# A mixer's score stage in another order: one cin chunk between the heads' and the sample's scores, exponentials before the v path on ScalarE

## The reference

```
ua, va, q, k, v, cin, gb, gc, gates = project(rmsnorm(x), w_in)
vn = rmsnorm(gelu(va), g_v)                     # the "v path" of branch A
A  = gelu(ua) * (W_s . vn + b_s)                # spatial mixing within 128 rows
B  = softmax(q k^T / 8 + relbias) v             # 8 heads of 64; the sample also sees its cache
C  = gb * causal_conv3(gc * cin)
x  = x + W_out(sum_b sigmoid(gates_b) * (branch_b @ W_branch_b))
```

## Time and profile before

| | us |
|---|---|
| median of 3 runs | 1827.11 |
| lowest, highest | 1825.47, 1828.17 |
| the profiled execution | 1827.44 |
| its span | 1825.7 |
| PE busy | 1789.3 (98%) |
| DVE busy | 1414.5 (77%) |
| ACT busy | 1098.5 (60%) |
| POOL busy | 72.8 (4%) |
| mean granted TensorE clock | 0.991 |

### The profile page before, as it was taken

How to read it: one execution, slowest core, us unless ns; L and a number is a source line. 1 busy time by engine, 2 the same in 40 slices (tenths; PEclk the granted TensorE clock), 3 DMA queues, 4 the chain that set the end, 5 groups by cost and what they waited for, 6 DMA issues and landing times.

```text
span 1825.7 us, 27550 instructions
## 1 busy us (share of the span) xinstructions
PE 1789.3 (98%) x10502; PEld 1596.2 (87%) x10502; DVE 1414.5 (77%) x1504; ACT 1098.5 (60%) x1068; POOL 72.8 (4%) x99
## 2 busy tenths in 40 slices
PE   9999999999999999999999999999999999999995
PEld 9899999999998999988888888888888888888884
DVE  6675667777765856779898788897888987988984
ACT  5444445333345344567777777777767777777773
POOL 2151000000000400000000000000000000000000
PEclk9999999999999999999999999999999999999998
DMA  9845554554544435469999999999999999999990
GB/s 340 276 148 183 172 161 162 175 172 147 177 144 138 148 119 174 139 213 368 373 366 342 332 358 354 372 354 323 365 324 388 364 345 331 357 359 368 349 365 26
DMA packets 253168, 487.06 MB, mean 267 GB/s; under 512 B 8160, under 2 KB 97280, under 8 KB 252784
## 3 DMA queue, kind: packets, MB, share of 16 engines
q1 hardware_dynamic: 248736, 467.87, 73.0%
q0 software_dynamic: 4304, 17.42, 2.8%
HBM read 477.38 MB, written 7.88 MB: 266 GB/s over the span
## 4 chain that ended last, share of the span: by engine, by line
issue 66%; PE 27%; DVE 3%; ACT 2%; POOL 1%; DMA 0%; SPq 0%; DVEq 0%; POOLq 0%
PE psum L1931 8%; PE psum L1933 8%; PE psum L1932 8%; POOL attn L789 1%; DVE w_lo L1150 1%; PE psum L1907 0%; PE psum L1906 0%; PE psum L1905 0%; ACT w_hi L821 0%; ACT attn L905 0%; DVE h_lo L1156 0%; DMA ring<-in_w_in 0%; DVE attn L1262 0%; PE psum L1745 0%; POOL attn L785 0%
## 5 line engine op out<-in xcount | busy, mean ns | idle before, releaser
L1438 DVE TENSOR_TENSOR e_lo<-ring,e_hi 128x2048 fp32r<-128x2048 f32 x224 | 511.5, 2289 | 77.1 <-ACT e_hi L1016 77.0
L1016 ACT ACTIVATE e_hi<-ring 128x2048 fp32r<-128x2048 f32 x224 | 429.8, 1919 | 162.9 <-PE psum L2045 162.9
L1150 DVE TENSOR_TENSOR w_lo<-ring,w_hi 128x1024 fp32r<-128x1024 f32 x218 | 267.1, 1230 | 165.2 <-ACT w_hi L821 163.5
L1931 PE MATMUL psum<-h_hi,w_hi 128*128 128x288 f32 x1248 | 373.6, 299 | 5.9 <-DVE w_lo L1150 3.0
L1932 PE MATMUL psum<-h_lo,w_hi 128*128 128x288 f32 x1248 | 370.1, 297 | 0.0
L1933 PE MATMUL psum<-h_hi,w_lo 128*128 128x288 f32 x1248 | 368.9, 296 | 0.0
L821 ACT ACTIVATE w_hi<-ring 128x1024 fp32r<-128x1024 f32 x218 | 230.0, 1057 | 212.6 <-PE psum L1933 191.7
L2043 PE MATMUL psum<-e_hi,he_hi 128*128 128x512 f32 x896 | 356.4, 398 | 0.2 <-ACT he_lo L1022 0.2
L2045 PE MATMUL psum<-e_hi,he_lo 128*128 128x512 f32 x896 | 351.8, 393 | 0.0
L2044 PE MATMUL psum<-e_lo,he_hi 128*128 128x512 f32 x896 | 351.8, 393 | 0.0
L1438 DVE TENSOR_TENSOR e_lo<-spare,e_hi 128x2048 fp32r<-128x2048 f32 x112 | 256.4, 2291 | 46.5 <-ACT e_hi L1016 46.0
(11 more groups left out here) (311 smaller groups left out, 2021.4 us busy)
## 6 DMA issues: line engine op xcount, KB each, us to landing
ring<-in_e_w SPq DMA_DIRECT2D x224, 1024.0 KB, 5.4
spare<-in_e_w SPq DMA_DIRECT2D x112, 1024.0 KB, 6.1
ring<-in_w_in SPq DMA_DIRECT2D x56, 1024.0 KB, 5.2
ring<-in_w SPq DMA_DIRECT2D x33, 1024.0 KB, 5.3
ring<-in_w_branch SPq DMA_DIRECT2D x12, 1024.0 KB, 5.0
ring<-in_w_out SPq DMA_DIRECT2D x8, 1024.0 KB, 5.2
bias_ext<-attn POOLq DMA_DIRECT2D x2, 2048.0 KB, 9.8
bias<-bias_ext POOLq DMA_DIRECT2D x2, 1536.0 KB, 11.9
```

The source lines that it names most:

```text
L1016: nc.scalar.activation(e_hi[split_buffer(c)][:, :], expert_ring[s][:, 0:PIECE_W], ACT.Copy).then_inc(piece_rounded, 1)
L1150: nc.vector.tensor_tensor(low, src, high.bitcast(f32), ALU.subtract).then_inc(split, 1)
L1438: nc.vector.tensor_tensor(e_lo[buf][:, :], expert_ring[s][:, 0:PIECE_W], e_hi[buf][:, :].bitcast(f32), ALU.subtract).then_inc(piece_split, 1)
L1931: nc.tensor.matmul(bank(name), high, src[0][:, k, :], start=(k == 0), stop=False)
```

## The change

In both layers, with nothing computed otherwise:

- PE computes cin chunk 0 right after the heads' scores; the sample's scores (now a function of their own), the transposes of va and cin chunks 1 to 3 follow. `mixer_groups` deals the banks in that order.
- ACT takes the exponentials before the v path. The pair "evacuate cin tile j, round gc chunk j" is spread: tile 0 after head 4, tile 1 after the sample's exponentials, tile 2 after the gelus, tile 3 after the squares. The wait for the stored state of the layer before moves ahead with them.
- DVE sets the bias mask before the va chunks, splits gc chunk 0 between the heads' maxima and the sample's scores, and gc chunks 1 to 3 before the norm of va instead of behind it.

```
-    g += [("s", l, h) for h in range(HEADS)] + [("s2", l, r) for r in range(2)]
-    g += [("vat", l, n) for n in range(3)]
-    g += [(s, l, j) for s in ("cin", "gc", "gb") for j in range(BT)]
+    g += [("s", l, h) for h in range(HEADS)] + [("cin", l, 0)] + [("s2", l, r) for r in range(2)]
+    g += [("vat", l, n) for n in range(3)] + [("cin", l, j) for j in range(1, BT)]
+    g += [(s, l, j) for s in ("gc", "gb") for j in range(BT)]
...
-                rows_evacuated("vat", l, vg, vg_ready, ACT.Gelu_apprx_tanh)
...
+                if l:
+                    act.wait_ge(state_stored, 32)
+
+                def cin_and_round(j):
+
+                    evacuate(("cin", l, j), z[:, j, 2:2 + TOK], P, TOK, cin_ready)
+                    round_lead(CHUNK_OF[("gc", l, j)])
 
                 for hd in range(HEADS):
                     act.wait_ge(top_ready, 9 * l + hd + 1)
...
                     ins.then_inc(exp_ready, 1)
+                    if hd == 4:
+                        cin_and_round(0)
...
-                if l:
-                    act.wait_ge(state_stored, 32)
-                for j in range(BT):
-                    evacuate(("cin", l, j), z[:, j, 2:2 + TOK], P, TOK, cin_ready)
-                    round_lead(CHUNK_OF[("gc", l, j)])
+                cin_and_round(1)
+                rows_evacuated("vat", l, vg, vg_ready, ACT.Gelu_apprx_tanh)
+                cin_and_round(2)
+                act.wait_ge(vg_ready, 3 * (l + 1))
...
+                cin_and_round(3)
+                act.wait_ge(vsq_ready, 3 * (l + 1))
...
+                    if s == "va":
+                        dve.wait_ge(bias_loaded, 16 * (l + 1))
+                        nc.vector.memset(bias[0:CHUNK, :, 256 + CHUNK:BIAS_W], MASKED).then_inc(bias_masked, 1)
...
-                dve.wait_ge(bias_loaded, 16 * (l + 1))
                 dve.wait_ge(ext_stored, 32)
-                nc.vector.memset(bias[0:CHUNK, :, 256 + CHUNK:BIAS_W], MASKED).then_inc(bias_masked, 1)
...
+                low_lead(CHUNK_OF[("gc", l, 0)])
                 dve.wait_ge(bias2_loaded, 16 * 8 * (l + 1))
...
+                for j in range(1, BT):
+                    low_lead(CHUNK_OF[("gc", l, j)])
                 dve.wait_ge(vrms_ready, 3 * (l + 1))
...
-                for j in range(BT):
-                    low_lead(CHUNK_OF[("gc", l, j)])
...
                 scores(l)
+                features("cin", l, [0])
+                sample_scores(l)
                 turn_rows("vat", l, va_t, va_scaled)
-                features("cin", l)
+                features("cin", l, range(1, BT))
```

More of the change, by code:

```diff
@@ L913, in _ @@
                 ins.then_inc(exp_ready, 1)
-                if l:
-                    act.wait_ge(state_stored, 32)
-                for j in range(BT):
-                    evacuate(("cin", l, j), z[:, j, 2:2 + TOK], P, TOK, cin_ready)
-                    round_lead(CHUNK_OF[("gc", l, j)])
+                cin_and_round(1)
+                rows_evacuated("vat", l, vg, vg_ready, ACT.Gelu_apprx_tanh)
+                cin_and_round(2)
+                act.wait_ge(vg_ready, 3 * (l + 1))
+                for n, (t0, rows) in enumerate(TILES):
+                    spare, at = GELU_BUFS[n]
+                    nc.scalar.activation(spare[0:rows, at:at + 2, 0:256], vg[0:rows, n, :].rearrange("p (a b) -> p a b", a=2),
+                                         ACT.Square, accum_out=vsq[0:rows, n:n + 1]).then_inc(vsq_ready, 1)
+                cin_and_round(3)
+                act.wait_ge(vsq_ready, 3 * (l + 1))
+                for n, (t0, rows) in enumerate(TILES):
+                    nc.scalar.activation(vrs[0:rows, n:n + 1], vsq[0:rows, n:n + 1], ACT.Sqrt, scale=1.0 / HALF,
+                                         bias=eps[0:rows, 0:1]).then_inc(vrms_ready, 1)
                 for j in range(BT):
@@ L1758, in scores, with sample_scores @@
                     give(nc.tensor.matmul(p[:, 128:384], q[:, 128:256], k[:, 0:256], start=True, stop=True))
+            def sample_scores(l):
                 for r in range(2):
```

## The result

The changed kernel takes **1832.19 us** (median of 20 runs, 1827.88 to 1839.51), the kernel before 1828.74 us in the runs beside it (20 runs, 1825.47 to 1832.35). The ratio is 1.0023, 95% interval 1.0014 to 1.0031: slower by about 3.5 us. The forecast was 1825.5 us, range 1821.0 to 1829.5, with 0.12 for slower. So the sign was wrong. Of the 6.7 us between forecast and result 1.6 are the base, since the median of before stood at 1827.11 when the forecast was made. The other 5.1 us are the change's.

A forecast was written before the change was run, and what follows sets the result against it. TensorE, busy 98% of the span, was taken as the bound, losing time to waits and half clock. Per layer 3.0 us won minus 2.2 lost gives 0.8, two layers 1.6: from the median 1825.5 us, range 1821.0 to 1829.5.

The forecast's parts named there:

- PE's side: Score stage on PE: waits for split weights gone, those at transposes under 0.3 us each, first gc chunk 6.2 us earlier.
- rival 2: Score stage keeps half rate, PE idles only 1.4 us before attention, clock stays up there: 1821.1 us; chance 0.14.
- The chain up to the convolution: ACT and DVE work from the heads' scores on: convolution starts at 114.9 instead of 118.28, 3.4 us earlier.
- 105.6 and 9.1: DVE: norm of va done at 105.6 us, then 9.1 us of work until the convolution starts, put at 114.9.
- The list for ACT: ACT's exponentials, evacuations with roundings, gelus, squares, roots and table loads in sequence, ending at 103.2 us.
- rival 4: Table switches on ACT cost 2.8 us a layer more, chain moves by 0.2: 1826.7 to 1831 us; chance 0.07.
- minus 0.4: Convolution on DVE: POOL's later scaling slows three steps, 4.0 against 3.6 us each, so the chain moves 3.0 us.
- the prediction's own sign: Wrong if attention's first value matmul moves by anything but 3 us, or the clock stays 1.00 in both places.
- PE's wait: PE reaches attention 5.9 us before the first value matmul: 2.1 us are transposes, 3.8 us idle.
- I bound what falls on the stage by 3.2 and 6.6 us: Half rate within the attention stage, costing 1.4 to 2.8 us a layer; 2.2 taken.
- Rival 3: Half rate lasts over the whole attention stage: 8.6 us lost against 3.0 won a layer, 1838.3 us; chance 0.09.
- slower from 7.0 us of half rate on: Attention stage: the change turns slower once half rate lasts 7.0 us, from 3.0/0.43.

The follow-up runs named there:

- changed, again: The changed kernel as it is, run once more for a second profile: 1831.61 us.
- fill13_late: Changed kernel with 13 extra matmuls between the last transpose and the first value matmul of the attention stage: 1825.23 us, ratio 0.9978 to the kernel before.
- defer: Changed kernel with ScalarE's two roundings of the next branch's weights moved behind the fourth copy of the attention stage: 1823.44 us, ratio 0.9960 to the kernel before.

## Why the prediction was wrong

- **PE's side: right.** The first gc chunk came 6.2 us earlier, the waits for split weights went. The waits at the transposes and cin chunk 1, 0.38 and 0.65 us, were a little longer than forecast. The clock was 1.00 near the scores, which the forecast wanted and rival 2 denied. The scores and transposes between two dense chunks did not bring it down once the waits were short.
- **The chain up to the convolution: right.** 3.4 us forecast, 3.6 measured. The forecast's own terms, 105.6 and 9.1, add up to 114.7 and not 114.9, a slip that changes nothing. The list for ACT held, with 1.28 us for each table load; rival 4 falls with it. Its second load lay hidden in ACT's wait, as assumed.
- **The chain through the convolution: undersized.** The step "minus 0.4" is the first that failed. It took POOL's scaling to lengthen each step by 0.4 us, for one step more than before. Measured were 17.0 us against 15.2: the steps took 4.46, 4.38, 4.37 and 3.81 us. Against 14.3 us with nothing beside it the contention costs 2.7 us, where before paid 0.8. I had the mechanism and priced it by a row in which other instructions were hit. So the mixing and the first value matmul moved by 1.8 us instead of 3.0, which by the prediction's own sign made it wrong; the run with the scaling early confirms this term, since there they moved by a further 2.6.
- **PE's wait: right in kind, 4.3 us instead of 3.8.**
- **The clock: right in place, undersized.** The step "I bound what falls on the stage by 3.2 and 6.6 us" is the second that failed. It took the length of a fall from one among dense chunks. In layer 0 of the two profiles of the changed kernel 5.9 and 3.5 us of half rate lay in the stage, inside these bounds; in layer 1 it was 9.6 and 9.7 us, beyond them (read off the windows, from the first value matmul to the return to 1.00). So the profiles lost 2.6, 4.3, 1.6 and 4.3 us in their four stages, 3.2 on the average, against 2.2 forecast, and 7.0 us is the most seen (18.5 us of stage in the kernel with ACT's and DVE's parts alone). Rival 3 described this, a half rate that the stage itself doesn't end, and I gave it 0.09, on the ground that the stage had held full clock for 11.4 us. That it holds a clock once granted said nothing of how soon it wins it back.
- **The sum.** Per layer 1.8 - 3.2 = 1.4 us lost, against 0.8 won. Twice the difference is 4.4 us of the 5.1 to be explained; the rest of 0.7 us I can't assign. Rival 3's own condition, "slower from 7.0 us of half rate on", rested on 3.0 us of gain. With 1.8 it is 4.2 us (1.8/0.43), which three of the four stages profiled exceed (their losses over 0.43: 6.1, 10.0, 3.7 and 10.1 us).

The Trainium skill (TensorE: Matmul & The Clock Gate, "Part 4: PE-mode transpose") says that transposes don't count as busy in the same way. I used it for the score stage, where the clock was 1.00. It fits better where I did not use it, in attention, whose transposes and matmuls of 32 to 128 columns kept the half rate for 12 us and more in two kernels (scaling early, layer 1; ACT's and DVE's parts alone) while PE was busy 3.00 of 3.00 us. But the same work also won it back after 3.5 us, so the sentence alone doesn't explain the length. No run here separates the transposes from the short matmuls.

What stays open: why the same wait of 1.95 to 2.65 us brings the clock down in some executions and not in others, how long the half rate then lasts, and whether the length of one wait or what follows it weighs more. With a wait of 1.95 us and dense matmuls between it and the first value matmul the clock held in both layers of the one profile (fill13_late), and without them it fell in both (defer). Behind a wait of 2.34 us with dense matmuls after it, it fell in one layer and held in the other.

## What to carry to other kernels

A lead won on the bounding engine is worth what the chain behind the next join moves, so follow that chain to the join, the engines beside it included: here moving GpSimd's scaling out of the convolution's way was worth 2.6 us a layer, more than the change brought the chain. What is left of the lead turns into a wait, and here waits of 1.95 to 2.65 us in front of short matmuls cost up to 7.0 us a layer in clock, more than the lead was worth. Remove the wait by shortening the chain (two roundings moved behind the fourth copy: 1.9 us a layer) before moving the engine that waits, and if one must stay, put dense matmuls between it and the short ones.

## What the runs showed of the hardware

- The half rate that a wait brings can last much longer over short matmuls and transposes than it did over dense chunks. Dense chunks had the full clock back 5.1 us after their first matmul (before, from 86.43 us) and 6.1 us after it (PE's part alone, from 102.15 us). Behind the first value matmul it took from 3.5 us (changed, again, layer 0) to 15.7 us (ACT's and DVE's parts alone). The clock was 0.50 through 12 us of a fully busy stage in one profile (GpSimd's scaling early, layer 1), one of its windows:

```profile
652.00:655.00 3.00, 3.00 (x17) 2.87 (x18) 0.00 (x0) 0.49 (x1) 0.00 (x0) 0.50 0.00 0
```

- Thirteen dense matmuls (1.7 us) between the transposes and the first value matmul were worth 6.4 us (1831.6 to 1825.2 us), and ahead of the transposes nothing (1831.6 us).
- GpSimd's scaling slows different DVE instructions in the two kernels (L1321 and the weight split before, L1323, L1325 and L1334 after). In both a convolution step beside it spans two heads of the scaling: 4.0 us with 16.01/8 = 2.0 us a head, and 4.4 with 17.84/8 = 2.2.
- The same program differs by up to 11.6 us from execution to execution (1827.88 to 1839.51 us), and its mean granted clock differs with it.
